# Products of the level scheme as two 64x64 blocks on column halves, and the samples' state updates by head on four row groups

## The chip, the core and the metric

The kernel runs on one core of a Trainium2 chip as one launch. The metric is the device time of the run in microseconds. TensorE multiplies, VectorE, ScalarE and GpSimd do the elementwise work, SyncE issues most of the transfers. SBUF holds 128 partitions; products land in eight PSUM banks of 512 float32 columns.

## What is computed

One step of a decoder layer for 512 prompt tokens and 8 samples of 4 tokens (544 tokens of width 1024), all in float32: a token mixer (a recurrent HGRN2 part of 4 heads and a short gated convolution, from one input projection), a normalisation, a mixture of 16 experts with two experts per token, and a normalisation. The recurrence, per head with keys and values of 128:

```python
S_t = diag(f_t) S_{t-1} + k_t v_t^T
o_t = S_t^T q_t
```

It is evaluated in chunks. The attention inside a chunk needs the product of decayed queries and keys for all causal pairs of tokens, and the state at the end of a chunk needs the sum of the decayed keys times the values. The samples start from given states, 8 x 4 matrices of 128x128, and return new ones.

## The kernel before

Every engine runs its own instruction list, written out by hand; semaphores order them. No planner is involved: the order of the work is the order in the source.

**Input projection with the level products.** The input weight comes in 14 chunks of 256 columns (`ORDER`: f, f, q, q, v, v, gc, gc, cx, cx, gb, gb, g, g). Each chunk is split into a high and a low part (ScalarE line 776, VectorE line 1073) and multiplied (lines 1644, 1651, 1652). Between the projections stand the pair products (`pairs`, lines 1667 to 1687). A prompt chunk has 128 tokens; the causal pairs of a chunk are split by binary levels. Level product 0 gives the diagonal; product `li` from 1 to 7 gives the pairs that lie in the two halves of a block of 2^li tokens, with queries and keys decayed to the middle of the block. Each is computed as a full 128x128 product for each of 4 heads and 4 chunks, and VectorE keeps what the level's mask selects (`take_pairs`, line 1136, a predicated copy). A head's four products fill one bank, and banks 4, 5 and 6 rotate: line 1683 waits until the head three places before was taken. Product `li` runs after projection `li + 4`.

The exponents of a level are made by GpSimd (lines 626 and 627), which waits until the products of the levels before are through, ScalarE exponentiates them (line 826), and VectorE multiplies them into the queries and keys (lines 1123 and 1124) behind the taking of the pairs and the split of the next weight chunk. In the steps of the chunks cx and gb VectorE also evacuates the projection's tiles (lines 1094 to 1114): a cx tile takes the whole convolution. In a VectorE step the order is: evacuate the projection two steps back, take the pairs, split the weights, multiply the decays.

After the last level the keys are decayed to the ends of their chunks (GpSimd line 636, ScalarE line 835, VectorE line 1180) and transposed by TensorE (lines 1717 and 1720); for the samples four transposes, one for each head, lay the 32 tokens on partitions 0 to 31.

**Output, mix and state updates.** The mixer's outputs are normalised per tile of 128 tokens and multiplied by the output weight in two halves of 512 columns, each in a convolution part and a recurrent part (`mix`, lines 1785 to 1806; the tile `tt = 4` holds the 32 sample tokens). The samples' state updates stand between the recurrent parts of the first half (lines 1828 to 1832). For head `h`, GpSimd spreads the values of the 32 sample tokens over 8 blocks, one for each sample, masked to that sample's rows (`mask_values`, line 658); TensorE multiplies the 32 key rows by four blocks at a time into banks 1 and 2 (line 1814), and VectorE adds the products to the decayed states (`new_states`, line 1280). There is one buffer of masked values, so the mask of the next head waits for the products of the one before (line 667). VectorE's order is: add the mix tile to the residual with its statistics, split weights where they are due (after tile 1), new states of the head. After the new states SyncE stores them (line 513) and goes on to the experts' weights. The second half of the mix (`last_mix`), the normalisation, the router and the experts follow.

## Time and profile before

| | |
|---|---|
| Time before, median of 3 runs | 677.18 us (675.67 to 677.30) |
| Profiled execution: its own time | 673.15 us |
| Profiled execution: span | 671.3 us |
| Mean granted TensorE clock | 0.985 |
| TensorE busy | 641.9 us, 96% of the span |
| VectorE busy | 513.9 us, 77% |
| ScalarE busy | 351.5 us, 52% |
| GpSimd busy | 147.1 us, 22% |

The profile is one execution. Times in rows are microseconds from the start of the span unless marked ns. PE is TensorE's matmul side, PEld its weight loads, DVE is VectorE, ACT ScalarE, POOL GpSimd, SP SyncE. A row names the line of the kernel, the operation, output and input, and the shape; `x32` counts records. A float32 product makes two matmul records, a transpose or a product of split (float32r) operands one. The projections take the span up to about 237 us, the mixer's outputs and the mix run to about 317, routing to about 350, the experts to about 660.

### The profile page before, as it was taken

The numbers are of one execution on the slowest core, as the hardware profiler recorded it, in microseconds if no ns is written. First come the engines' busy times: TensorE is split into PE (matmuls) and PEld (weight loads), VectorE is DVE, ScalarE is ACT, GpSimd is POOL, SyncE is SP. The second block draws the span as 40 slices with busy tenths as digits, with TensorE's granted clock in tenths as the row PEclk, the third lists the DMA queues.
The fourth block names the chain that finished last, engine by engine and source line by source line (L and its number), as shares of the span: only waits on it lengthen the run. The fifth ranks groups of instructions, "written<-read, shape, count | busy, mean of one in ns | idle before, by whom it ended". The sixth has DMA issues, their size and how long they took to land.

```text
span 671.3 us, 9632 instructions
## 1 busy us (share of the span) xinstructions
PE 641.9 (96%) x3809; PEld 544.5 (81%) x3809; DVE 513.9 (77%) x599; ACT 351.5 (52%) x353; POOL 147.1 (22%) x81
## 2 busy tenths in 40 slices
PE   8999999988999999999979999999999999999894
PEld 6999899988997897578857888888888888888641
DVE  4326446699767376877679999999999999999887
ACT  4538423322226162012506877877777777777732
POOL 0000514422221330400020211122212222200657
PEclk9999999999999999999779999999999999999998
DMA  9972112111612205089249999999999999998443
GB/s 289 380 291 64 63 63 64 63 63 63 188 63 63 85 17 201 0 276 410 75 148 351 355 411 408 414 418 395 413 412 406 409 419 406 401 413 326 137 164 133
DMA packets 48994, 163.16 MB, mean 243 GB/s; under 512 B 4342, under 2 KB 23626, under 8 KB 36668
## 3 DMA queue, kind: packets, MB, share of 16 engines
q1 hardware_dynamic: 42092, 137.22, 54.0%
q0 software_dynamic: 6864, 25.43, 10.0%
q8 instruction: 25, 0.41, 0.3%
q14 instruction: 13, 0.11, 0.0%
HBM read 142.67 MB, written 19.96 MB: 242 GB/s over the span
## 4 chain that ended last, share of the span: by engine, by line
PE 86%; DVE 8%; ACT 2%; POOL 1%; issue 1%; DMA 1%; SPq 0%; DVEq 0%
PE bank L1922 25%; PE bank L1934 13%; PE bank L1651 7%; PE bank L1652 7%; PE bank L1804 5%; PE bank L1644 5%; PE bank L1686 4%; PE bank L1912 2%; PE bank L2026 1%; PE bank L1884 1%; PE bank L1839 1%; PE bank L1944 1%; PE bank L1814 1%; PE bank L2038 1%; PE bank L1615 1%; PE bank L1616 1%
## 5 line engine op out<-in xcount | busy, mean ns | idle before, releaser
L1439 DVE TENSOR_TENSOR RA<-FA,RA 128x2048 fp32r<-128x2048 f32 x93 | 212.7, 2289 | 20.8 <-ACT RA L929 20.2
L929 ACT ACTIVATE RA<-FA 128x2048 fp32r<-128x2048 f32 x93 | 179.0, 1925 | 41.5 <-PE bank L1922 25.5
L1922 PE MATMUL bank<-RA 128*128 128x512 f32 x768 | 184.9, 395 | 2.9 <-DVE RA L1444 2.0
L1922 PEld LDWEIGHTS bank<-RA 128*128 128x128 f32 x768 | 141.0, 188 | 34.0 <-DVE RA L1444 2.4
L1651 PE MATMUL bank<-RA 128*128 128x272 f32 x432 | 109.1, 290 | 0.0
L1652 PE MATMUL bank<-RA 128*128 128x272 f32 x432 | 108.5, 288 | 0.0
L1934 PE MATMUL bank<-RA 128*128 128x512 f32 x384 | 89.9, 390 | 1.4 <-DVE RA L1449 1.4
L1934 PEld LDWEIGHTS bank<-RA 128*128 128x128 f32 x384 | 72.0, 188 | 16.6 <-DVE RA L1449 1.6
L1651 PEld LDWEIGHTS bank<-RA 128*128 128x128 f32 x432 | 81.5, 189 | 0.0
L1652 PEld LDWEIGHTS bank<-RA 128*128 128x128 f32 x432 | 81.4, 188 | 0.0
L1073 DVE TENSOR_TENSOR RA<-FA,RA 128x2048 fp32r<-128x2048 f32 (+1 forms) x18 | 48.6, 2699 | 26.6 <-ACT RA L776 26.2
L776 ACT ACTIVATE RA<-FA 128x2048 fp32r<-128x2048 f32 (+1 forms) x18 | 33.6, 1868 | 50.0 <-PE bank L1652 26.3
L673 POOL DMA_INDIRECT FA<-x_by_token,ids x16 | 39.1, 2447 | 74.8 <-DVE ids L1397 58.4
L690 POOL DMA_DIRECT2D y_by_slot<-FA x14 | 8.1, 579 | 212.0 <-DVE FA L1456 212.0
L1644 PE MATMUL bank<-RA 128*128 128x256 f32 x384 | 47.1, 283 | 0.0
L1644 PEld LDWEIGHTS bank<-RA 128*128 128x128 f32 x384 | 46.1, 188 | 1.2 <-issue 0.7
L1804 PE MATMUL bank<-RA 128*128 128x512 f32 x192 | 47.0, 398 | 0.0
L1804 PEld LDWEIGHTS bank<-RA 128*128 128x128 f32 x192 | 35.5, 188 | 10.2 <-issue 2.3
L626 POOL TENSOR_TENSOR FA<-FA 128x1024 f32<-128x1024 f32 (+1 forms) x7 | 16.6, 2368 | 109.1 <-PE bank L1686 65.8
L826 ACT ACTIVATE FA<-FA 128x2048 f32<-128x2048 f32 (+1 forms) x7 | 13.6, 1947 | 49.4 <-POOL FA L627 49.4
L1686 PE MATMUL bank<-FA 128*128 128x128 f32 x256 | 30.7, 277 | 3.9 <-DVE FA L1136 3.9
L1686 PEld LDWEIGHTS bank<-FA 128*128 128x128 f32 x256 | 29.4, 192 | 4.4 <-DVE FA L1136 4.3
(271 smaller groups left out, 800.8 us busy)
## 6 DMA issues: line engine op xcount, KB each, us to landing
FA<-w_up SPq DMA_DIRECT2D x32, 1024.0 KB, 7.4
FA<-w_gate SPq DMA_DIRECT2D x32, 1024.0 KB, 7.0
FA<-w_down SPq DMA_DIRECT2D x32, 1024.0 KB, 7.9
FA<-w_in SPq DMA_DIRECT2D x13, 1024.0 KB, 5.1
y_by_slot<-FA POOLq DMA_DIRECT2D x14, 512.0 KB, 7.6
y_by_slot<-FA POOLq DMA_DIRECT2D x1, 5120.0 KB, 21.6
FA<-w_out SPq DMA_DIRECT2D x4, 1024.0 KB, 5.1
FA<-x_prompt SPq DMA_DIRECT2D x8, 256.0 KB, 5.1
```

The costliest lines, as they stand in the source:

```text
L673: pool.indirect_dma_start(out=xg[par], out_offset=None, in_=x1_dram, in_offset=bass.IndirectOffsetOnAxis(ap=ids[:, bi:bi + 1].bitcast(U32) ...
L776: nc.scalar.activation(split[o % 2][0][:, cs], raw[o % 3][:, cs], ACT.Copy).then_inc(s_hi, 1)
L929: nc.scalar.activation(split[split_slot(bi, j)][0], raw[place], ACT.Copy).then_inc(m_hi, 1)
L1073: tt_(split[o % 2][1][:, cs], raw[o % 3][:, cs], f(split[o % 2][0][:, cs]), ALU.subtract).then_inc(s_lo, 1)
L1439: tt_(sl[1], raw[place], f(sl[0]), ALU.subtract).then_inc(m_lo, 1)
L1644: last = mm(pb[:, 0:CW], xT[x_][:, kt, tok(j)], w_[:, kt, :], start=(kt == 0 and i == 0), stop=(kt == KT - 1 and i == 2))
L1651: mm(pb[:, 0:HT], lhs, xT[x_][:, kt, 0:HT], start=first, stop=end)
L1652: last = mm(ps[:, 0:HT], lhs, xT[x_][:, kt, HT:T], start=first, stop=end)
L1686: last = mm(bank[4 + p % 3][:, cols], lf[:, h, cols], rf[:, h, cols], start=True, stop=True)
L1804: last = mm(w_bank(half, tt)[0:rows, :], xT[x_][:, k0 + kt, tok(tt)], w_[:, kt, :], start=(conv and kt == 0 and i == 0), stop=(not conv an ...
L1922: last = mm(out[:, :], xgT[par][x_][:, kt, :], w[w_][:, t, :], start=(kt == 0 and i == 0), stop=(kt == KT - 1 and i == 2))
L1934: last = mm(bank[5 + g][:, :], hT[x_][:, kt, :], w[w_][:, t, 512 * g:512 * g + 512], start=(kt == 0 and i == 0), stop=(kt == 3 and i == 2))
```

## The change

The level products 1 to 6 are made of two 64x64 products per chunk: the first 64 tokens against themselves, written to partitions 0 to 63, and the last 64, written to partitions 64 to 127. Product 7 is one 64x64 product (first half's keys, second half's queries). Product 0 is unchanged. What is not written in the bank is not selected by the masks.

The samples' keys and values are laid out by head on four groups of 32 partitions: the decayed sample keys are multiplied into a separate buffer (`k_end`), so that one transpose turns all heads; ScalarE copies the values of heads 1 to 3 to partitions 32 to 127; one masking instruction on GpSimd covers all heads. The eight products of the update (head `n % 4`, sample half `n // 4`) go to banks 1, 2 and 6 in turn and are issued in groups of 3, 3 and 2 after the mix tiles 1, 2 and 3. TensorE gets two new waits: for all tiles of the mixer's output before the first group, and for six of the new states before the second half of the mix, which uses bank 6.

```diff
--- before.py
+++ after.py
@@ -111,7 +111,7 @@
     c[:, C_IO:C_IO + P] = np.arange(P)[None, :]
     s[:, SM_G4:SM_G4 + TOPG] = TOPG - np.arange(TOPG)
     s[:, SM_VAL:SM_VAL + NTT] = (np.arange(NTT)[None, :] * P + p[:, None]) < T
-    s[:, SM_SEQ:SM_SEQ + DB] = (p[:, None] // DS) == np.arange(DB)[None, :]
+    s[:, SM_SEQ:SM_SEQ + DB] = (p[:, None] % NS // DS) == np.arange(DB)[None, :]
     c[:, C_QM:C_QM + DB * NS] = (np.arange(NS)[None, :] // DS == np.arange(DB)[:, None]).reshape(1, -1)
     m = np.zeros((P, LEVELS, P), np.float32)
     for l in range(LEVELS):
@@ -187,7 +187,7 @@
 
         k_tok = fa(E0 + H * T, H * NC * P).rearrange("p (h c k) -> p h c k", h=H, c=NC)
         state = fa(E0, NC * H * P).rearrange("p (c h v) -> p c h v", c=NC, h=H)
-        k_tok_s = fa(Q0 + H * T, 512).rearrange("p (h k) -> p h k", h=H)
+        k_tok_s, k_end = fa(Q0 + H * T, P), fa(E0 + H * T + H * NC * P, P)
         v_msk = fa(Q0 + H * T + 512, DB * P).rearrange("p (b v) -> p b v", b=DB)
         h_gain, h_gain_s = fa(Q0 + H * T + 1536, 512), fa(Q0 + H * T + 2048, P)
         B0 = Q0 + 2 * H * T
@@ -247,7 +247,7 @@
         s_kt, s_ktc = sem("k_transposed"), sem("k_token_major")
         s_su, s_st, s_o = sem("state_update"), sem("state_ready"), sem("o_made")
         s_x2, s_fold = sem("x_tail_ready"), sem("tail_rows_folded")
-        s_vm, s_sus, s_s0n, s_sto = sem("v_masked"), sem("sample_update"), sem("sample_state"), sem("sample_states_stored")
+        s_vm, s_sus, s_s0n, s_sto = sem("v_by_head_and_masked"), sem("sample_update"), sem("sample_state"), sem("sample_states_stored")
         s_stp = sem("prompt_state_stored")
         s_selt, s_sel = sem("groups_transposed"), sem("groups_t_ready")
         s_csq, s_cms, s_crt, s_crc, s_cbc = (sem("conv_squares"), sem("conv_mean_square"), sem("conv_root"),
@@ -377,6 +377,12 @@
         def o_width(tt):
 
             return H * P if tt < 4 else P
+
+        UPDATE_UNITS = (range(0, 3), range(3, 6), range(6, 8))
+
+        def update_bank(n):
+
+            return bank[(1, 2, 6)[n % 3]]
 
         def w_bank(half, tt):
 
@@ -652,20 +658,14 @@
             pool.wait_ge(s_eva, len(act_tiles) + 1)
             nc.gpsimd.tensor_tensor(sg[:, 4, 0:P], sg[:, 4, 0:P], h_gain_s, ALU.mult).then_inc(s_sg, 1)
 
-            seq_mask = small[0:NS, SM_SEQ:SM_SEQ + DB].unsqueeze(2).broadcast_to([NS, DB, P])
-
-            def mask_values(h):
-                nc.gpsimd.tensor_tensor(v_msk[0:NS], v_tok[0:NS, 4, h * P:(h + 1) * P].unsqueeze(1).broadcast_to([NS, DB, P]),
-                                        seq_mask, ALU.mult).then_inc(s_vm, 1)
-
+            seq_mask = small[:, SM_SEQ:SM_SEQ + DB].unsqueeze(2).broadcast_to([P, DB, P])
             pool.wait_ge(s_fold, 2)
-            mask_values(0)
+            pool.wait_ge(s_vm, 1)
+            nc.gpsimd.tensor_tensor(v_msk, v_tok[:, 4, 0:P].unsqueeze(1).broadcast_to([P, DB, P]), seq_mask,
+                                    ALU.mult).then_inc(s_vm, 1)
             pool.wait_ge(s_stp, 16)
             pool.wait_ge(s_o, NTT)
             nc.gpsimd.memset(xr[:, 4, :], 0.0).then_inc(s_xr0, 1)
-            for h in range(1, H):
-                pool.wait_ge(s_sus, 2 * h)
-                mask_values(h)
 
             def gather(bi, par):
 
@@ -825,6 +825,10 @@
                     n = T if l < SLEVELS else SEQ
                     nc.scalar.activation(ex[l % 2][:, :, 0:n], ex[l % 2][:, :, 0:n], ACT.Exp).then_inc(s_e, 1)
                 if o == 9:
+                    act.wait_ge(s_fold, 2)
+                    for h in range(1, H):
+                        last = nc.scalar.activation(v_tok[h * NS:(h + 1) * NS, 4, 0:P], v_tok[0:NS, 4, h * P:(h + 1) * P], ACT.Copy)
+                    last.then_inc(s_vm, 1)
                     act.wait_ge(s_selt, 1)
                     act.wait_ge(s_b, H)
                     nc.scalar.activation(const[0:8, C_RST:C_RST + 4 * P], bank[7][0:8, :], ACT.Copy).then_inc(s_sel, 1)
@@ -1177,13 +1181,14 @@
                     nc.vector.tensor_copy(p_decay, ex[1][:, :, P - 1:SEQ:P])
                     link(nc.vector.tensor_copy(s0_decay.rearrange("p (b h) -> p h b", h=H), ex[1][:, :, SEQ + DS - 1:T:DS]))
                     dve.wait_ge(s_e, LEVELS + 2)
-                    tt_(k[:, :, :], k[:, :, :], ex[0][:, :, :], ALU.mult).then_inc(s_kx, 1)
+                    tt_(k_end.rearrange("p (h t) -> p h t", h=H), k[:, :, SEQ:T], ex[0][:, :, SEQ:T], ALU.mult)
+                    tt_(k[:, :, 0:SEQ], k[:, :, 0:SEQ], ex[0][:, :, 0:SEQ], ALU.mult).then_inc(s_kx, 1)
 
                     for h in range(H):
                         dve.wait_ge(s_kt, h + 1)
                         nc.vector.tensor_copy(k_tok[:, h, :, :], bank[4 + h % 2][:, :].rearrange("p (c k) -> p c k", c=NC)).then_inc(s_ktc, 1)
                     dve.wait_ge(s_kt, H + 1)
-                    nc.vector.tensor_copy(k_tok_s[0:NS], bank[4][0:NS, :].rearrange("p (h k) -> p h k", h=H)).then_inc(s_ktc, 1)
+                    nc.vector.tensor_copy(k_tok_s, bank[4][:, 0:P]).then_inc(s_ktc, 1)
 
             dve.wait_ge(s_crt, 2)
             nc.vector.reciprocal(r_conv, r_conv).then_inc(s_crc, 1)
@@ -1271,14 +1276,15 @@
                 nc.vector.bn_stats(stats[:, tt, 6 * half:6 * half + 6], xr[:, tt, cols]).then_inc(s_dv, 1)
                 chain[0] += 1
 
-            def new_states(h):
-
-                for g in range(2):
-                    dve.wait_ge(s_sus, 2 * h + g + 1)
+            def new_states(units):
+
+                for n in units:
+                    h, g = n % H, n // H
+                    dve.wait_ge(s_sus, n + 1)
                     for i in range(4):
                         bi = 4 * g + i
                         last = stt(s0[:, bi, h, :], s0[:, bi, h, :], s0_decay[:, bi * H + h:bi * H + h + 1],
-                                   bank[1 + g][:, i * P:(i + 1) * P], ALU.mult, ALU.add)
+                                   update_bank(n)[:, i * P:(i + 1) * P], ALU.mult, ALU.add)
                     last.then_inc(s_s0n, 1)
 
             dve.wait_ge(s_o, NTT)
@@ -1290,8 +1296,8 @@
                 add_mix(0, tt)
                 if tt == 1:
                     lo(NCH + 2)
-                if tt < H:
-                    new_states(tt)
+                if tt in (1, 2, 3):
+                    new_states(UPDATE_UNITS[tt - 1])
             lo(NCH + 3)
             dve.wait_ge(s_lnp, 32)
             for tt in range(NTT):
@@ -1681,9 +1687,17 @@
                     p = li * H + h
                     if p >= 3:
                         pe.wait_ge(s_pc, p - 2)
+                    to = bank[4 + p % 3]
                     for c in range(NC):
                         cols = slice(c * P, (c + 1) * P)
-                        last = mm(bank[4 + p % 3][:, cols], lf[:, h, cols], rf[:, h, cols], start=True, stop=True)
+                        first, second = slice(c * P, c * P + P // 2), slice(c * P + P // 2, (c + 1) * P)
+                        if li == 0:
+                            last = mm(to[:, cols], lf[:, h, cols], rf[:, h, cols], start=True, stop=True)
+                        elif li < LEVELS:
+                            mm(to[0:P // 2, first], lf[:, h, first], rf[:, h, first], start=True, stop=True)
+                            last = mm(to[P // 2:P, second], lf[:, h, second], rf[:, h, second], start=True, stop=True)
+                        else:
+                            last = mm(to[0:P // 2, second], lf[:, h, first], rf[:, h, second], start=True, stop=True)
                     last.then_inc(s_p, 1)
 
             for o_ in range(NCH):
@@ -1716,8 +1730,7 @@
                             for c in range(NC):
                                 last = tr(bank[4 + m % 2][:, c * P:(c + 1) * P], k[:, m, c * P:(c + 1) * P], ident)
                         else:
-                            for h in range(H):
-                                last = tr(bank[4][0:NS, h * P:(h + 1) * P], k[:, h, SEQ:T], ident)
+                            last = tr(bank[4][:, 0:P], k_end, ident)
                         last.then_inc(s_kt, 1)
 
                     pe.wait_ge(s_csq, 1)
@@ -1805,13 +1818,15 @@
                                   start=(conv and kt == 0 and i == 0), stop=(not conv and kt == 3 and i == 2))
                 last.then_inc(s_w, 1)
 
-            def sample_updates(h):
-
-                pe.wait_ge(s_vm, h + 1)
-                for g in range(2):
-                    if h:
-                        pe.wait_ge(s_s0n, 2 * h + g - 1)
-                    mm(bank[1 + g][:, :], k_tok_s[0:NS, h, :], v_msk[0:NS, 4 * g:4 * g + 4, :],
+            def sample_updates(units):
+
+                pe.wait_ge(s_vm, 2)
+                pe.wait_ge(s_ol, NTT)
+                for n in units:
+                    if n >= 3:
+                        pe.wait_ge(s_s0n, n - 2)
+                    rows, g = slice((n % H) * NS, (n % H + 1) * NS), n // H
+                    mm(update_bank(n)[:, :], k_tok_s[rows, :], v_msk[rows, 4 * g:4 * g + 4, :],
                        start=True, stop=True).then_inc(s_sus, 1)
 
             pe.wait_ge(s_cl, 5)
@@ -1828,8 +1843,8 @@
             for tt in range(NTT):
                 pe.wait_ge(s_ol, tt + 1)
                 mix(0, False, tt)
-                if tt < H:
-                    sample_updates(tt)
+                if tt in (1, 2, 3):
+                    sample_updates(UPDATE_UNITS[tt - 1])
 
             def logits(tt):
 
@@ -1860,6 +1875,7 @@
                     pe.wait_ge(s_wc, tt)
                 mix(1, conv, tt)
 
+            pe.wait_ge(s_s0n, 6)
             for n in range(6):
                 last_mix(n)
             pe.wait_ge(s_s0n, 2 * H)
```

## Rows read from the trace of the kernel before

**Rows 1.** The page: busy time of the engines; granted TensorE clock in 40 slices.

```profile
PE 641.9 (96%) x3809; PEld 544.5 (81%) x3809; DVE 513.9 (77%) x599; ACT 351.5 (52%) x353; POOL 147.1 (22%) x81
...
PEclk9999999999999999999779999999999999999998
```

**Rows 2.** Waits of TensorE, 60 to 345 us: total us, times, longest us.

```profile
PE bank L1686 <- DVE FA L1136: 3.9, 2, 2.0
...
PE bank L1637 <- ACT FA L788: 2.0, 2, 1.6
```

**Rows 3.** Chain that ended last, 90 to 345: start us, us, engine, line, records.

```profile
110.25 0.37 PE bank L1679 x8
110.62 3.77 PE bank L1686 x32
...
126.41 3.57 PE bank L1686 x32
...
147.07 1.16 PE bank L1686 x8
...
214.26 0.61 PE bank L1720 x4
...
247.44 1.88 PE bank L1782 x64
```

**Rows 4.** Timeline of TensorE's weight loads, 246.5 to 250: start us, us, line, shape.

```profile
247.01 0.15 PEld L1779 LDWEIGHTS bank<-FA 32*32 32x32 f32 x8
```

**Rows 5.** Timeline of VectorE, 76 to 250: start us, us, [idle before, releaser].

```profile
127.34 0.74 DVE L1136 COPY_PREDICATED FA<-masks,bank 128x512 f32<-128x512 uint8 x1 [4.62 <-PE bank L1686]
...
130.79 3.45 DVE L1073 TENSOR_TENSOR RA<-FA,RA 128x2048 fp32r<-128x2048 f32 x1
...
142.51 0.06 DVE L1094 MEMSET FA<- 128x2 f32 x1 [0.45 <-PE bank L1652]
...
146.30 2.71 DVE L1136 COPY_PREDICATED FA<-masks,bank 128x512 f32<-128x512 uint8 x4
...
179.01 0.74 DVE L1136 COPY_PREDICATED FA<-masks,bank 128x512 f32<-128x512 uint8 x1
...
212.07 1.29 DVE L1184 COPY FA<-bank 128x512 f32<-128x512 f32 x2 [3.80 <-PE bank L1717]
```

**Rows 6.** Timeline of ScalarE, 76 to 250.

```profile
142.54 1.91 ACT L776 ACTIVATE RA<-FA 128x2048 fp32r<-128x2048 f32 x1 [4.12 <-PE bank L1652]
...
203.38 2.03 ACT L835 ACTIVATE FA<-FA 128x2176 f32<-128x2176 f32 x1 [5.78 <-POOL FA L636]
...
240.58 1.27 ACT L854 ACTIVATE FA<-FA 32x128 f32<-32x128 f32 x4
```

**Rows 7.** Timeline of VectorE, 246 to 328, at the state updates.

```profile
272.87 0.69 DVE L1266 SCALAR_TENSOR_TENSOR FA<-FA,bank 128x512 f32<-128x512 f32 x1 [1.44 <-PE bank L1804]
...
274.20 2.27 DVE L1073 TENSOR_TENSOR RA<-FA,RA 128x2048 fp32r<-128x2048 f32 x1
276.39 2.15 DVE L1280 SCALAR_TENSOR_TENSOR FA<-FA,bank 128x128 f32<-128x128 f32 x8
```

**Rows 8.** Chain that ended last, 90 to 345, state updates and mix.

```profile
267.92 1.91 PE bank L1814 x4
...
283.24 1.91 PE bank L1814 x4
...
287.14 16.70 PE bank L1804 x72
```

**Rows 9.** Stretches of 1 us: length, busy us by engine, clock, DMA share, GB/s.

```profile
335.00:336.00 1.00, 0.54 (x3) 0.12 (x1) 0.86 (x5) 0.00 (x0) 0.00 (x0) 1.00 0.00 0
337.00:338.00 1.00, 0.13 (x5) 0.13 (x5) 1.00 (x4) 0.00 (x0) 0.00 (x0) 0.76 0.00 0
339.00:340.00 1.00, 0.95 (x11) 0.90 (x12) 0.37 (x2) 0.00 (x0) 0.00 (x0) 0.50 0.00 0
344.00:345.00 1.00, 1.00 (x5) 0.82 (x4) 1.00 (x2) 0.00 (x0) 1.00 (x1) 0.83 0.82 283
```

## The prediction

> **What bounds the kernel now.** I read the page first: TensorE is busy for 96% of the span, no other engine for more than 77%, and the granted clock is full except in one stretch near the middle [rows 1]. So I looked for the places where TensorE waits ahead of the expert loop. There are few: twice about 2 us in the level products, on VectorE's taking of the level before, and 1.6 us on a ScalarE evacuation [rows 2]. The chain of waits through both changed stages is therefore made of TensorE's own instructions, and work taken from them comes off the end unless VectorE is late next. That question decides the sum.
>
> A float32 product shows as two matmul records. A head of a level (four 128x128 products) is 8 records, a level 32 records in 3.57 us, 112 ns each [rows 3]. Products of 32 columns to the four column groups of one bank run closer: 64 records in 1.88 us, 29 ns each, although each streams the same 128 columns [rows 3]. Four column groups of one row group thus run side by side.
>
> **Part 1, the level products.** Levels 1 to 6 now issue two 64x64 products per chunk, 64 records; the last level one, 32 records; the diagonal stays. No row shows 64 columns. From below, a record streams half of 128 columns, 56 ns, and two halves side by side give 28 ns a record, nearly what the four groups show. From above, records of 32 columns that all go to one column group take 0.37 us for 8, 46 ns [rows 3]; twice the columns would be 92 ns. I take 29 ns, because the nearest rows alternate column groups as the change does, and their weight loads overlap too: eight loads to four groups of one row group lie within 0.15 us [rows 4]. A level is then 64 x 29 ns = 1.88 us. The last one sends 32 records to one half, so I take 56 ns each, 1.8 us.
>
> The Trainium skill, TensorE: Matmul & The Clock Gate, section on packing small matmuls, has weight loads overlap running matmuls only where the row group differs, which the two halves do not. The overlapping loads above speak against it; by that rule the sum would be the slower rival below.
>
> Now VectorE. Three banks rotate, so TensorE's fourth head waits until VectorE has taken the first.
> - Products 1 to 3. VectorE starts its first take 0.04 us after the first head's 8 x 112 ns [rows 3, 5], later about 0.6 us after the level's start; TensorE resumed 0.77 us after such a take began (146.30 to 147.07 [rows 3, 5]). The fourth head may start at 1.37, before the third ends (1.41). A level is 1.9 us, a gain of 1.65, three times: 4.95. VectorE's four takes, 0.68 each back to back, end 1.0 us earlier, and it had 0.45 us to spare ahead of the next tile [rows 5], about covering the 1.65.
> - Products 4 and 5 follow the cx tiles. VectorE is still on the convolution there, runs without a gap, and TensorE stands before the fourth head. Only that head shrinks, 1.16 to 0.74 us with its drain [rows 3]: 0.42 twice, 0.84.
> - Products 6 and 7 follow the gb tiles; the first take starts when VectorE is through them (179.01 [rows 5]), the fourth head at 179.78, the end at 180.25. Now such a level starts 0.93 us before its first take (126.41 and 127.34 [rows 3, 5]), so it ends at 179.01 - 0.93 + 3.57 = 181.65: 1.4 twice, 2.8.
>
> That is 8.6. Changing the product's width may cost something: levels that follow 32-column products show 3.77 against 3.57 [rows 3]. Between 0 and 0.2 us for seven levels I take 0.15, 1.0 in all. **7.6 us** are left.
>
> Behind the last level GpSimd's subtraction starts; ScalarE's exponential waits 5.78 us for it, then squares, and only then evacuates the tile for which TensorE waited 1.6 us [rows 2, 6]. This chain moves with TensorE. GpSimd is slowed while VectorE splits weights beside it (both then stretch: 3.45 us for a split [rows 5], 2.27 elsewhere [rows 7]), and it now has some 0.6 us more ahead of that split, since VectorE is still taking pairs: between 0 and 0.6, I take **0.4**. Four transposes of sample keys become one; three fewer at 0.11 (0.61 for four, with a lead-in [rows 3]) give **0.3**. VectorE multiplies the 128 sample columns apart from the rest: one instruction more, hidden because VectorE then waits 3.80 us for TensorE's transposes of the result [rows 5]; without that cover some 0.2. ScalarE's three copies of values (four like them took 1.27 us [rows 6], so about 1.0) sit in its queue before the copy of the group table and the weight rounding of the next chunk; there it waits 4.12 us for a cx tile [rows 6], so nothing, and at most 1.0 without that. GpSimd's wait for them ends long before it gets there.
>
> **Part 2, the state updates.** Now each head costs TensorE 1.91 us for two products [rows 8], four times. Between the first update's start, 267.92, and the second half of the mix, 287.14, lie 19.2 us. The first mix tile (12 records in 2.78 us, as 72 in 16.70 [rows 8]) would end at 270.7, no update ahead of it. Three products on three row groups follow. No row shows row groups side by side; alone a product is 0.95, so three lie between 0.95 and 2.85; I take 1.05, because the column groups overlap fully: 271.75. The next mix ends at 274.55. Then VectorE is late: sum and statistics 1.33 us, a weight split 2.19, and 1.07 for a unit's four state rows (2.15 for eight) [rows 7]. From 270.75 the first three units are free at 275.35, 276.4 and 277.5. The next three products want those banks, so they go one by one to 278.55. A new wait of about 0.8 us arises before the first, with the next mix queued behind it. Mix to 281.35, two products 1.0, the short tail tile 2.0 (283.24 + 1.91 to 287.14 [rows 8]): the second half starts at 284.35, **2.8 us** earlier. Its new wait, on six units, ends near 282.2. The weights for its third tile are split by about 290, when they are needed: this is late next. GpSimd's 3 masks are gone; one with 128 partitions takes its first one's place ahead of the residual's loads. The new wait for all mixer rows is over before the first mix tile ends. The state store, on SyncE's queue ahead of the expert weights, moves earlier by about 1 us, less than what reads them, but they are wanted only after the routing.
>
> **The clock.** In the two cx levels TensorE finishes three heads in 1.4 us instead of 2.7 and stands still for some 3.2 us instead of 2.0. In the routing it now idles from about 335.5; within 337 to 338 the granted clock falls (0.76 on average) to the lower of its levels, 0.50 or 1.2 GHz; dense work runs from about 339.5, and full speed, 2.4 GHz, comes back in 344 to 345 [rows 9]. Some 5 us of dense work at half speed lose 2.5 us. The two gaps of 2.0 us in the levels did not drop it [rows 1]. Between no drop and two (0 and 5.0) I take one: **-2.5**.
>
> **The sum.** 7.6 + 0.4 + 0.3 + 2.8 - 2.5 = 8.6 us. Against the profiled run's own 673.15 us (span 671.3) that is 664.55. The median shown, 677.18, stands 4.0 above that run; the predicted median is 677.18 - 8.6 = 668.6.
>
> **The rivals.**
> - The halves follow one another, loads hidden: four records of 56 ns a chunk, 224, as now. Levels 1 to 6 gain nothing, no gap grows, only the last level's 1.4 stays: 1.4 + 0.4 + 0.3 + 2.8 = 4.9, 672.3. Against it: 29 ns in [rows 3]. 0.10.
> - Slower: the halves share one row group, the load of the second cannot start under the first, and every record costs 92 ns. A level of 64 records is 5.9 us, 2.3 more. Four levels (1, 2, 3 and 6) bound by TensorE give 9.2, the fourth heads of the two cx levels 2 x 0.6, the last level (2.9) gains 0.6; less 3.5 from the rest: 6.3 slower, 683.5. It decides from about 70 ns a record, where the levels' loss eats the 3.5. For it: 46 ns in one column group; against it: the overlapping loads [rows 4]. 0.04.
> - The row groups do not overlap: 1.05 + 2.85 - 2.1, about 1.7 less from the updates: 670.3. 0.08.
> - The clock falls in more places (both gaps, the wait in the updates, and beyond): four falls of 2.5 leave 11.1 - 10 = 1.1 us, 676.1, no measurable change. 0.05.
> - The change does not do what it says, the stage being set by VectorE throughout: the 0.45 us that VectorE has to spare in one place and the 4.62 in another [rows 5] speak against that. Only the updates gain: 674. 0.03.
>
> **How the numbers follow.** The forecast, with none to two falls, has 0.70. 0.3% of 677.18, about what a measurement of this kernel can tell from no change, is 2.0 us. Faster: the forecast, the hidden-load case, the row groups and most of the last case, 0.90; same 0.06; slower 0.04. The range: no fall and no cost of width give 11.1 + 1.0 = 12.1, 665.1, and the runs spread 1.5 below their median, so 664.0; at the top 672.3 with the row groups also failing, 674, cut to 673.5.
>
> **What would show it.** Right: records of the level products near 29 ns and levels near 1.9 us; TensorE's wait on VectorE's takes at about 3 us twice; one mask on GpSimd; a wait of about 0.8 us on new states before the fourth update product, and later products one by one; the mix's second half 16.4 us after the first mix tile. Wrong: level products at 3.6 us or more; the granted clock at 0.50 after more than two places; TensorE waiting for cx or gb evacuations where it ran through; the second half waiting for its weights.

## The result, and the profile after

The changed kernel takes 670.17 us in the median of four runs (669.29 to 671.23), the kernel before beside it 677.05 (675.67 to 677.30): 6.9 us less. The ratio is 0.9909, with an interval of 0.9884 to 0.9934, which is 4.5 to 7.9 us. The forecast was 8.6 less, 668.6 us; the time is in its range, though 8.6 itself lies above that interval. One execution of the experiments below, of the kernel with the updates alone, took 1059.89 us at a granted clock of 0.555 and enters no ratio.

The two profiled executions are closer than the medians: 671.23 us (span 669.4) after and 673.15 (span 671.3) before. A second profile of the kernel before, from the experiments below, is longer: 677.22 us (span 675.4). First the page of the kernel after, TensorE's busy time and its granted clock in 40 slices:

```profile
PE 638.1 (95%) x3998; PEld 539.6 (81%) x3998; DVE 510.1 (76%) x600; ACT 352.7 (53%) x356; POOL 138.8 (21%) x78
...
PEclk9999999978999999899789999999999999999997
```

The busy shares are within a point of those of before, but the clock is now below full in two places ahead of the slice where it fell before [rows 1]. The level products come next: the line view of the kernel after, first the two halves of level 1 in a window around it, then the last level, which has one half (record durations min/median/max in ns, first and last start in us).

```profile
L1697 PE MATMUL bank<-FA x32: 222/222/271, 95.2 to 97.2; 128*64 128x64 f32 x32
...
L1700 PE MATMUL bank<-FA x32: 222/222/270, 192.8 to 194.8; 128*64 128x64 f32 x32
```

In level 1 the other half's 32 records (line 1698) lie between these: 64 records start within 2.0 us, 32 ns apart. In the last level 32 records that all go to one half start within the same 2.0 us, 64 ns apart. So two halves take the time of one. The 32 and 64 ns are means. The timelines of level 1 show what is in them, first TensorE's records (start, duration), then VectorE's takes:

```profile
95.72 0.22 PE L1697 MATMUL bank<-FA 128*64 128x64 f32 x1
95.73 0.22 PE L1698 MATMUL bank<-FA 128*64 128x64 f32 x1
95.78 0.22 PE L1697 MATMUL bank<-FA 128*64 128x64 f32 x1
...
96.60 0.22 PE L1698 MATMUL bank<-FA 128*64 128x64 f32 x1
96.75 0.27 PE L1697 MATMUL bank<-FA 128*64 128x64 f32 x1
```

```profile
95.94 2.61 DVE L1140 COPY_PREDICATED FA<-masks,bank 128x512 f32<-128x512 uint8 x4 [0.18 <-PE bank L1698]
```

In a run a pair of records, one for each half, starts every 58 ns, which is 29 ns a record. The fourth head starts at 96.75, 0.15 us behind the last record of the third and 0.81 us after VectorE's first take began. On the chain, level 1 lasts from 95.28 to 97.43, 2.15 us, against 3.57 to 3.77 before [rows 3]. This is what TensorE waits for:

```profile
PE bank L1697 <- DVE FA L1140: 6.2, 2, 3.1
...
PE bank L1643 <- ACT FA L788: 1.9, 2, 1.6
...
PE bank L1829 <- DVE FA L1286: 0.8, 1, 0.8
```

The two waits on VectorE's takes have grown from 3.9 us in all [rows 2] to 6.2, 3.1 each; the wait on ScalarE's evacuation has stayed; the wait on new states is new and has the 0.8 us forecast. The chain of the kernel after, in the stretches that the change touches:

```profile
192.83 2.22 PE bank L1700 x32
...
212.03 0.33 PE bank L1733
...
262.60 5.59 PE bank L1817 x24
...
272.99 3.10 PE bank L1829 x6
276.09 4.54 PE bank L1817 x12
280.63 1.06 PE bank L1829 x4
...
283.68 16.69 PE bank L1817 x72
```

One transpose of sample keys stands where four did [rows 3]; three products on three row groups, 268.10 to 269.17 in the trace, take 1.07 us, then VectorE is late and the next three go one by one in 3.10. The mix tile behind them takes 4.54 us for 12 records; the first two tiles, 24 records at 262.60, take 5.59, 2.8 each. The 1-us stretches say why (columns: busy shares of PE, PEld, DVE, ACT and POOL with their records, granted clock, DMA share, GB/s):

```profile
143.00:144.00 1.00, 0.24 (x4) 0.24 (x6) 1.00 (x4) 0.00 (x0) 0.00 (x0) 0.66 0.00 0
...
149.00:150.00 1.00, 1.00 (x7) 1.00 (x6) 1.00 (x2) 0.00 (x0) 1.00 (x1) 0.50 0.00 0
...
276.00:277.00 1.00, 1.00 (x4) 0.84 (x4) 1.00 (x5) 0.00 (x0) 0.00 (x0) 0.72 0.00 0
...
279.00:280.00 1.00, 1.00 (x4) 0.77 (x3) 0.33 (x2) 0.00 (x0) 0.00 (x0) 0.57 0.00 0
```

Towards the end of each 3.1-us wait the clock falls from full (2.4 GHz) to 0.50 (1.2 GHz). Worked out from the means of the first and last stretch of each fall, it is low from 143.3 to 150.1, from 163.8 to 167.2 and from 276.4 to 279.9; the last lies within the mix tile just named, with TensorE busy.

To see where the time went, I cut every trace at the first starts of the same lines, read to 0.1 us: product 0's sample part, the transposes behind product 3 and behind product 7, the first prompt state update, the samples' outputs, the first transpose of the normalised residual, the first transpose of gathered tokens. Microseconds from each cut to the next, the last one to the end of the span:

| stretch | before | before again | after |
|---|---|---|---|
| start to product 0 | 76.6 | 76.9 | 77.4 |
| products 0 to 3 | 53.2 | 53.3 | 49.1 |
| products 4 to 7 | 67.3 | 68.8 | 68.5 |
| behind product 7 | 39.9 | 39.9 | 39.5 |
| prompt states | 10.4 | 10.4 | 10.4 |
| outputs, mix, updates | 56.3 | 57.8 | 55.3 |
| residual to routing | 44.6 | 44.6 | 46.1 |
| experts and rest | 323.0 | 323.7 | 323.1 |

Products 0 to 3 gain 4.1 us, nearly the 4.5 worked out. Products 4 to 7, which should gain 3, lose 1.2 us against the first profile, and the updates give 1.0 instead of 2.8. Both are where the clock fell.

### The profile page after: what moved, and what is told of

It reads as the page before. It is cut to its first block, busy times and chain, and to the rows that moved or that the text cites. A ratio compares the mean times of both kernels' runs of the same rounds, so it can differ in the third digit from the quotient of the medians.

```text
span 669.4 us, 10013 instructions
## 1 busy us (share of the span) xinstructions
PE 638.1 (95%) x3998; PEld 539.6 (81%) x3998; DVE 510.1 (76%) x600; ACT 352.7 (53%) x356; POOL 138.8 (21%) x78
## 4 chain that ended last, share of the span: by engine, by line
PE 83%; DVE 9%; ACT 3%; POOL 2%; DMA 1%; issue 1%; SPq 1%; DVEq 0%
PE bank L1938 25%; PE bank L1950 13%; PE bank L1657 8%; PE bank L1658 7%; PE bank L1817 6%; PE bank L1650 4%; PE bank L1928 2%; PE bank L1854 2%; PE bank L1697 1%; PE bank L2042 1%; PE bank L1960 1%; PE bank L1900 1%; PE bank L2054 1%; DMA FA<-x_prompt 1%; PE bank L1621 1%; POOL FA L642 1%
## 5 line engine op out<-in xcount | busy, mean ns | idle before, releaser
L1938 PEld LDWEIGHTS bank<-RA 128*128 128x128 f32 x768 | 141.0, 188 | 34.1 <-DVE RA L1450 2.4
L1657 PE MATMUL bank<-RA 128*128 128x272 f32 x432 | 112.2, 295 | 0.0
L1658 PE MATMUL bank<-RA 128*128 128x272 f32 x432 | 111.2, 293 | 0.0
L1950 PEld LDWEIGHTS bank<-RA 128*128 128x128 f32 x384 | 73.1, 191 | 17.0 <-DVE RA L1455 1.6
L1657 PEld LDWEIGHTS bank<-RA 128*128 128x128 f32 x432 | 83.8, 194 | 0.5
L1658 PEld LDWEIGHTS bank<-RA 128*128 128x128 f32 x432 | 83.7, 194 | 0.0
L673 POOL DMA_INDIRECT FA<-x_by_token,ids x16 | 39.5, 2469 | 107.1 <-DVE ids L1403 91.6
L776 ACT ACTIVATE RA<-FA 128x2048 fp32r<-128x2048 f32 (+1 forms) x18 | 33.6, 1867 | 50.6 <-PE bank L1658 27.7
L1650 PEld LDWEIGHTS bank<-RA 128*128 128x128 f32 x384 | 46.1, 188 | 1.2 <-issue 1.2
L1817 PEld LDWEIGHTS bank<-RA 128*128 128x128 f32 x192 | 36.6, 194 | 10.0 <-issue 1.5
L632 POOL TENSOR_TENSOR FA<-FA 128x1024 f32<-128x1024 f32 (+1 forms) x7 | 16.6, 2368 | 107.5 <-PE bank L1698 64.2
L938 ACT ACTIVATE RA<-bank 128x512 fp32r<-128x512 f32 x32 | 17.2, 593 | 16.3 <-PE bank L1928 16.3
L1140 DVE COPY_PREDICATED FA<-masks,bank 128x512 f32<-128x512 uint8 x28 | 18.4, 727 | 9.3 <-PE bank L1698 9.3
```

The costliest lines, as they stand in the source:

```text
L673: pool.indirect_dma_start(out=xg[par], out_offset=None, in_=x1_dram, in_offset=bass.IndirectOffsetOnAxis(ap=ids[:, bi:bi + 1].bitcast(U32) ...
L776: nc.scalar.activation(split[o % 2][0][:, cs], raw[o % 3][:, cs], ACT.Copy).then_inc(s_hi, 1)
L1140: nc.vector.copy_predicated(att[:, h, :, :], m, src).then_inc(s_pc, 1)
L1650: last = mm(pb[:, 0:CW], xT[x_][:, kt, tok(j)], w_[:, kt, :], start=(kt == 0 and i == 0), stop=(kt == KT - 1 and i == 2))
L1657: mm(pb[:, 0:HT], lhs, xT[x_][:, kt, 0:HT], start=first, stop=end)
L1658: last = mm(ps[:, 0:HT], lhs, xT[x_][:, kt, HT:T], start=first, stop=end)
```

## The experiments

The theory: the parts do what the forecast says, and the falls of the clock take it back, above all those that the two longer waits bring. The rivals: the halves cost more than their records show, or the falls cost nothing, since other engines set the end of these levels. A gain below is one less the ratio, times the median of the kernel before as measured beside it; by this measure the change itself gains 6.2 us.

### Fill the two waits

TensorE makes twelve products that nothing reads, into the idle bank 7, ahead of the fourth head of products 4 and 5.

```diff
+                    if h == 3 and li in (4, 5):
+                        pe.wait_ge(s_sel, 1)
+                        filler = RA[:, 32 * K + KT * T:32 * K + KT * T + 640]
+                        for _ in range(12):
+                            mm(bank[7][:, :], filler[:, 512:640], filler[:, 0:512], start=True, stop=True)
                     if p >= 3:
```

> The changed kernel, with 12 products of no use (512 columns, into the idle bank 7) ahead of the fourth head of level products 4 and 5, where TensorE otherwise stands for 3.1 us. Theory 'clock': the gaps are what drops the granted clock there (6.4 and 3.3 us at the lower level in the changed kernel's profile, some 3.2 + 1.6 us lost); with the gaps filled the clock stays full from 130 to 180 us, the projections behind levels 4 and 5 start no later than 0.3 us after VectorE's first take, and the run is some 4 to 5 us faster than the changed kernel (670.2), so 665 to 666. Rival 'VectorE': that stretch is as long as VectorE needs, whatever the clock; then the run stays within 1 us of 670.

Measured: 665.42 us, ratio 0.9833 [0.9810, 0.9856], a gain of 11.3 us, 4.8 us under the median of the change. In its 1-us stretches, at the place of the first wait:

```profile
143.00:144.00 1.00, 0.93 (x5) 0.43 (x3) 0.97 (x5) 0.00 (x0) 0.00 (x0) 1.00 0.00 0
144.00:145.00 1.00, 0.93 (x18) 0.86 (x19) 1.00 (x3) 0.00 (x0) 0.15 (x1) 1.00 0.00 0
```

The clock stays full through all levels. Products 4 to 7 take 64.3 us instead of 68.5: the edit adds work to TensorE and takes none away, and the stretch is 4.2 us shorter. The two falls were the cause. The fall in the updates is still there (271.2 to 278.0; that stretch takes 57.0), and is not touched by this edit.

### Each part alone, and the halves in turn

Three kernels, measured together with the last one: the kernel before with only the level products of the change; the change with the level products of before (the loop of four 128x128 products per head); and the change with all first halves of a head ahead of all second halves:

```diff
                         elif li < LEVELS:
-                            mm(to[0:P // 2, first], lf[:, h, first], rf[:, h, first], start=True, stop=True)
-                            last = mm(to[P // 2:P, second], lf[:, h, second], rf[:, h, second], start=True, stop=True)
+                            last = mm(to[0:P // 2, first], lf[:, h, first], rf[:, h, first], start=True, stop=True)
...
+                    if 0 < li < LEVELS:
+                        for c in range(NC):
+                            second = slice(c * P + P // 2, (c + 1) * P)
+                            last = mm(to[P // 2:P, second], lf[:, h, second], rf[:, h, second], start=True, stop=True)
```

> The kernel before with the 64x64 level products alone (the state updates as before). Theory 'clock': levels 1 to 3 take 2.15 us each instead of 3.6 to 3.8, the clock falls in the two gaps, 8 us gained and up to 5 lost: 3 to 5 us faster than before, 672 to 674. Rival: the gain of the change came from the updates alone; then within 1 us of 677.

> The changed kernel with the level products as full 128x128 blocks again, so that the state updates alone are changed. Theory 'clock': the updates give 2.8 us (16.4 us from the end of the first recurrent mix tile to the second half of the mix, 19.2 before) where the clock holds through VectorE's wait and the three products one by one, and 1.0 where it falls there as in the changed kernel: 1 to 3 us faster than before, 674 to 676. Rival 'levels alone': no gain, within 1 us of 677.

> The changed kernel, with the four products of a head's first half issued before the four of its second half (levels 1 to 6), the same products in another order. Theory 'side by side': halves overlap only where they alternate; a record then takes 56 ns or more and a level 3.6 us, as in the kernel before, the gaps in levels 4 and 5 shrink to about 2 us, and the levels' gain is gone: 672 to 675. Rival 'shorter products': a level stays near 2.15 us, because 64 columns stream faster than 128, and the time stays at 670.

Measured: the levels alone 669.73 us, ratio 0.9905 [0.9875, 0.9936], a gain of 6.4; the updates alone 670.76, 0.9926 [0.9899, 0.9952], 5.0; the halves in turn 669.79, 0.9917 [0.9887, 0.9946], 5.6. All three gain more than I expected. By stretch:

| stretch | levels only | updates only | halves in turn | gaps filled |
|---|---|---|---|---|
| products 0 to 3 | 49.1 | 53.3 | 50.6 | 49.0 |
| products 4 to 7 | 65.8 | 68.8 | 68.4 | 64.3 |
| behind product 7 | 39.8 | 39.6 | 39.5 | 39.5 |
| outputs, mix, updates | 57.8 | 53.8 | 53.8 | 57.0 |

The chain of the kernel with the updates alone, at the place shown above for the change:

```profile
267.04 5.58 PE bank L1809 x24
...
277.43 3.10 PE bank L1821 x6
280.52 2.98 PE bank L1809 x12
283.51 1.06 PE bank L1821 x4
...
286.56 15.55 PE bank L1809 x67
```

The same products, and the mix tile now takes 2.98 us: where the clock holds, the updates gain 2.5 (53.8 against 56.3), here and in the halves in turn. Where it falls beside the old updates, as with the levels alone (from 275 on) and in the second profile of before, the stretch is 57.8, and the gain against that would be 4.0. The parts together gain less than the two alone (6.2 against 6.4 + 5.0); in the profiles each of the two was spared a fall that the whole has. Elsewhere in this profile the updates alone gain only 0.3, behind product 7; their 5.0 [3.2 to 6.8] is more than these 2.8 together. That the old updates often meet a fall, and so lose more than the first profile shows, would explain it, but how often was not measured.

The levels alone show that a long wait does not bring a fall every time. Their profile has the same two waits as the change (140.35 to 143.43 and 157.88 to 160.96); a line of its waits and a 1-us stretch behind the first:

```profile
PE bank L1691 <- DVE FA L1136: 6.2, 2, 3.1
```

```profile
144.00:145.00 1.00, 1.00 (x11) 0.96 (x8) 1.00 (x2) 0.00 (x0) 0.79 (x1) 1.00 0.00 0
```

The clock stays full behind the first wait and is low only behind the second, from 162.5 to 165.9; products 4 to 7 take 65.8 us, 1.5 more than with the gaps filled, where the two falls of the change cost 4.2. In the profile of the updates alone, with the waits of before (2.0 us), it is low from 148.7 to 152.1, behind the first of them.

The halves in turn missed what I expected. Its line view, level 1:

```profile
L1697 PE MATMUL bank<-FA x32: 221/222/272, 95.6 to 97.8; 128*64 128x64 f32 x32
L1703 PE MATMUL bank<-FA x32: 221/222/271, 95.8 to 98.1; 128*64 128x64 f32 x32
```

64 records start within 2.5 us, about 40 ns apart, though eight in a row go to the same half; one half alone has 64 ns in the mean. The start of its timeline there:

```profile
95.55 0.50 PE L1697 MATMUL bank<-FA 128*64 128x64 f32 x5
95.84 0.27 PE L1703 MATMUL bank<-FA 128*64 128x64 f32 x1
95.89 0.22 PE L1697 MATMUL bank<-FA 128*64 128x64 f32 x1
```

In the list of instructions the second half's first record (line 1703) stands behind eight of the first half; in the trace it starts behind five, ahead of the sixth. They overlap without being issued one by one in turn, at a price: 0.5 us a level, 1.5 for three levels (50.6 against 49.1). What in the engine lets them is not shown by any of these runs. The whole comes out at the time of the change: in its profile the waits are shorter (2.6 us), the falls in the levels too (146.2 to 149.6 and 166.7 to 170.1), and the updates are spared.

### Two groups of four updates

With the gaps filled, the updates go in two groups of four row groups, to banks 1, 2, 6, 7 and 1, 2, 4, 5; the second group stands behind the mix's tail, its new states behind the last weight split.

```diff
-        UPDATE_UNITS = (range(0, 3), range(3, 6), range(6, 8))
+        UPDATE_UNITS = (range(0, 4), range(4, 8))
...
-            return bank[(1, 2, 6)[n % 3]]
+            return bank[(1, 2, 6, 7, 1, 2, 4, 5)[n]]
...
             lo(NCH + 3)
+            new_states(UPDATE_UNITS[1])
...
-                if tt in (1, 2, 3):
-                    sample_updates(UPDATE_UNITS[tt - 1])
+                if tt in (1, 4):
+                    sample_updates(UPDATE_UNITS[tt // 4])
```

> The changed kernel with the two gaps of the level products filled, and with the eight update products in two groups of four, all four row groups at once: the first four behind the second recurrent mix tile (banks 1, 2, 6, 7), the other four behind the tail tile (banks 1, 2, 4, 5), the new states of the second four behind the last weight split. Theory 'banks': TensorE's wait of 0.8 us and the three products one by one (3.1 us) come from having three banks; with four and five a group takes 1.1 us, nothing waits, the second half of the mix starts some 13 us after the end of the first recurrent mix tile (16.5 in the changed kernel at full clock), so 2 to 4 us faster than with the gaps filled alone (665.4): 661 to 664. Rival 'VectorE': the new states only move behind the split, the normalisation waits for VectorE, and the time stays at 665.

Measured: 660.28 us, ratio 0.9775 [0.9743, 0.9806], a gain of 15.2, 3.9 more than with the gaps filled alone. Its chain:

```profile
258.45 5.57 PE bank L1823 x24
264.01 1.07 PE bank L1836 x8
...
272.69 1.09 PE bank L1836 x8
273.79 16.91 PE bank L1823 x72
```

Four products cost what three cost (1.07), none waits, and no fall comes before 310. The stretch of the mix and updates takes 49.8 us, 4.0 less than the 53.8 of the three-group order where the clock holds. Between the end of the first mix tile (258.45 and half of 5.57) and the second half lie 12.6 us: three tiles at 2.8 to 2.9, the tail 1.8, and 2.2 for all eight products. The updates alone had 16.7 there (269.83 to 286.56): the difference is VectorE's being late, the wait and the products one by one.

### Four banks for the levels; the kernel before with its gaps filled; the kernel before again

Four banks instead of fillers, with the updates in two groups as before: products 4 to 6 rotate over banks 4 to 7, so that the fourth head no longer waits.

```diff
+        def pair_bank(p):
+
+            return bank[4 + (p % 4 if 4 * H <= p < 7 * H else p % 3)]
```

The filled kernel before has the filler of the first experiment with seven products instead of twelve, for its shorter waits; the third kernel is the one before, unchanged.

> The updates as in the run with two groups, and no filler: instead the level products 4 to 6 rotate over four banks (bank 7 too), so that TensorE need not wait for VectorE's first take. Theory 'clock and VectorE': the 3.1 us gaps go, and the next projection starts 3 us earlier, but VectorE is busy without a break in the two cx steps, so TensorE waits elsewhere (for an evacuated cx tile, for decays), some 2 us twice; the stretch to the end of level 7 gets 1 to 3 us shorter than with filled gaps where the clock holds: 659 to 664. Rival: the waits only move and drop the clock as before: 664 to 667.

> The kernel before, with 7 products of no use ahead of the fourth head of level products 4 and 5, where its gaps are 2.0 us. Theory 'clock': its profile shows full clock there, but other executions may have lost it (the updates alone, with the same level products, showed one fall of 3.4 us there): 0 to 3 us faster than before, 674 to 677, and full clock from 130 to 180 us. Rival: the clock is no matter in the kernel before: within 1 us of 677.

> The kernel before, once more, for a second profile of it. Theory 'clock': the one profile shown is one of its faster executions (673.15 against a median of 677); a second one shows the clock falling in places where the first does not, in the gaps of the level products, the updates or the last experts, some 1.7 us for each. Rival: the same falls as in the first, and the profile's own time near 673.

Measured with four banks: 659.05 us, ratio 0.9754 [0.9724, 0.9785], a gain of 16.6. The two waits are gone without fillers, but another has come in their place. The largest of TensorE's waits:

```profile
PE bank L1709 <- DVE FA L1132: 3.9, 2, 3.7
```

Two 1-us stretches of the same kernel, in that wait and at its end:

```profile
169.00:170.00 1.00, 0.00 (x0) 0.00 (x0) 1.00 (x2) 1.00 (x1) 0.00 (x0) 1.00 0.00 0
...
171.00:172.00 1.00, 0.20 (x4) 0.20 (x6) 1.00 (x2) 0.00 (x0) 0.00 (x0) 0.50 0.63 238
```

TensorE now stands 3.7 us before product 6, until VectorE has multiplied its decays, and the clock falls there, from 170.2 to 177.0. Products 4 to 7 take 63.8.

The kernel before with its gaps filled: 674.53 us, ratio 0.9997 [0.9975, 1.0019]. No change that can be measured: products 4 to 7 take 67.3, as in the first profile. Filling pays where waits bring the clock down. Those of 2.0 us did not in the first profile; in the profile of the updates alone and in the next one a fall stands behind one of the two. What that leaves to gain on average is within the interval, from 1.3 us lost to 1.7 gained.

The kernel before again: 675.73, ratio 0.9996 [0.9967, 1.0026], single runs 671.69 to 679.49. In its profile the clock is low in three places where the first profile of before has it full, 166.2 to 169.6, 282.3 to 285.7 and 640.7 to 644.1; stretches from the first two:

```profile
168.00:169.00 1.00, 1.00 (x6) 1.00 (x6) 1.00 (x1) 0.00 (x0) 1.00 (x2) 0.50 0.00 0
...
283.00:284.00 1.00, 1.00 (x4) 0.78 (x3) 0.85 (x4) 0.00 (x0) 1.00 (x1) 0.50 0.00 0
```

Each of these two cost 1.5 us (68.8 against 67.3, and 57.8 against 56.3 in the table), and the last stretch, with the third, is 0.7 longer: 3.7 of the 4.1 us between the two profiled executions. So falls come in some executions of the kernel before and not in others, and the profile on which the prediction stood was one with few. That explains most of the 4.0 us by which it lies under its median. The first pair of profiles shows 1.9 us where the medians show 6.9 for this reason and because the profiled execution of the change was the slowest of its four, 1.1 above their median.

### Four banks, and the new wait filled

```diff
+                    if li == 6:
+                        pe.wait_ge(s_pc, 6 * H)
+                        filler = RA[:, 32 * K + KT * T:32 * K + KT * T + 640]
+                        for _ in range(13):
+                            mm(bank[7][:, :], filler[:, 512:640], filler[:, 0:512], start=True, stop=True)
                     pe.wait_ge(s_z, li)
```

> The run with four banks, with 13 products of no use ahead of level product 6, where TensorE stands for 3.7 us and the granted clock fell for 6.8 us behind it. Theory 'clock': the fall goes, the end of level 7 comes 2 to 3 us earlier (112.8 us after the start of level product 0 in the run with four banks, 110 to 111 here), and the run takes 656 to 657.5 us against 659. Rival 'VectorE': that stretch is bound by VectorE whatever the clock, the end of level 7 stays, and the time stays at 659.

Measured: 656.22 us (655.75 to 658.04), ratio 0.9716 [0.9690, 0.9741], a gain of 19.2: the best of all, ahead of both kernels. The wait before product 6 is down from 3.7 us to 0.8 and the fall there is gone; from the waits of TensorE:

```profile
PE bank L1714 <- DVE FA L1132: 0.8, 1, 0.8
```

Products 4 to 7 take 61.5 us, 2.3 less than with four banks alone (63.8); the gains differ by 2.6. The first fall of the clock is at 307.

## Why the prediction was right or wrong

- **The level products: right.** I took 29 ns a record from the column groups of 32, and in a run it is 29. With the 0.15 us for the change of width a level was to be 2.03, and is 2.15. That the 0.15 nearly fits is partly luck, since no run shows a cost of width by itself, and about half of what was added comes with the fourth head. I let it start 1.37 us into the level, without a pause; it starts at 1.55 (95.20 to 96.75), after a pause of 0.15, which fits VectorE's first take, begun 0.74 us into the level and not 0.6. The 46 ns behind the slower rival were a mean of eight records; in the trace the last seven of them start 32 ns apart. The last level was to be 1.95 with its width and is 2.22 on the chain: 58 ns a record in a run, not 56, and a pause of 0.21 before its fourth head. Products 1 to 3 were to gain 4.5 with the width taken off (4.95 - 0.45) and gain 4.1; 4 to 7 were to gain 3.0 (0.84 + 2.8 - 0.6) and gain 3.0 where the clock holds (67.3 to 64.3). 7.1 to 7.2 against 7.6. The rivals in which the halves go one after another, or all loads are exposed, are out. The Trainium skill, TensorE: Matmul & The Clock Gate, section on packing small matmuls, lets loads overlap running products only where the row group differs. By it two halves would cost twice one half; the trace disagrees, 32 ns a record with two halves against 64 with one.
- **Behind the last level: half right.** The transposes came (0.33 instead of 0.61). The 0.4 on GpSimd's subtraction did not: its two instructions take 6.01 us in both kernels. I also put TensorE's wait in the wrong place: the 1.6 us on ScalarE [rows 2] stand before product 0, at 73.0 to 74.6. Behind the last level TensorE waits much less for ScalarE, here in windows of 190 to 220, before and after:

```profile
PE bank L1637 <- ACT FA L788: 0.4, 1, 0.4
```

```profile
PE bank L1643 <- ACT FA L788: 0.3, 1, 0.3
```

The stretch goes from 39.9 to 39.5, 0.4 for a forecast of 0.7: 0.28 from the transposes and 0.13 from this wait (0.43 to 0.30).
- **The copies and the split multiplication: right, hidden.** ScalarE's three copies took 0.95 us at 134.60, beside a wait. VectorE's extra multiplication took 0.29 at 203.63; VectorE waits 3.7 us behind it.
- **The updates: right in the mechanism, 2.5 for 2.8.** Row groups overlap (1.07 for three, I took 1.05), the wait is 0.8, the products behind it go one by one, and the second half starts 16.7 us after the first mix tile where the clock holds (the updates alone), for 16.4 forecast and 19.2 before. In the profiled execution of the change only 1.0 of it was left, because the clock fell within a mix tile.
- **The clock: the step that failed.** I took one fall of 2.5 us between none and two, because the 2.0-us waits of before had not dropped it. In the profiled execution of the change both of the new 3.1-us waits dropped it, and the two together cost 4.2 us, as the filled kernel shows; with the levels alone the same two waits brought one fall and 1.5 us. So the length of a wait does not settle whether the clock falls. A third fall, in the updates, cost 1.5 in this execution, beside products that kept TensorE busy; I had no term for it. With three places ahead of the routing at 0.50, a sign that I had named for being wrong came true. The bound of 5.0 held for the levels, but not the value.
- **The reference for the sum.** I took the difference from the profiled run and carried it to the median, as if the two differed by a constant. They differ by falls, which are part of what the change moves. In medians the change gains 6.9: of the terms without the clock, 4.1 + 3.0 + 0.4 + 2.5 = 10.0 for the forecast 11.1, some 3 are given back. Against the profiled run the sum gave 664.55, and the profiled execution of the change took 671.23, 6.7 more. That the median came within 1.6 us of the forecast is therefore partly luck: the kernel before loses to falls in its median too, which the sum did not know. The case of more falls, at 676.1 with a chance of 0.05, was the right direction and too far.

Which executions have a fall, in the levels or in the updates, what starts it in the updates with TensorE busy, and what moves the falls in the routing (317 in the change, 323 before) and near 635, was not tried and stays open. The stretch that holds the former is 1.5 us longer in the profile of the change (46.1 against 44.6).

## What to carry to other kernels

Price a change that makes TensorE faster twice: by what it saves, and by the waits that it lengthens, since a wait can lower the clock for work that the change does not touch, in some executions and not in others. Where a wait cannot be removed, products that nothing reads can hold the clock; where a spare bank removes it, look for the wait that takes its place. Profile the kernel before more than once before its falls, or their absence, go into a sum.

## What the runs showed that was not expected

VectorE and GpSimd do not slow one another a little, as I had read [rows 5, 7]; by the rows below they take turns. VectorE's timeline in the kernel after, behind the first long wait (start, duration, line, output and input, shapes):

```profile
145.70 3.40 DVE L1077 TENSOR_TENSOR RA<-FA,RA 128x2048 fp32r<-128x2048 f32 x1
149.02 2.91 DVE L1127 TENSOR_TENSOR FA<-FA 128x1024 f32<-128x1024 f32 x1
```

GpSimd's timeline there:

```profile
144.97 1.97 POOL L632 TENSOR_TENSOR FA<-FA 128x1024 f32<-128x1024 f32 x1 [12.35 <-PE bank L1698]
146.91 3.94 POOL L633 TENSOR_TENSOR FA<-FA 128x1024 f32<-128x1024 f32 x1
```

The split ends 2.2 us after GpSimd's first instruction (146.94 to 149.10); GpSimd's second ends 1.75 us after the split (150.85); VectorE's decay ends 1.1 us after that (151.93). Each is close to the length that the instruction has elsewhere, 2.27 [rows 7], 1.89 and 1.21, and 0.1 shorter. The Trainium skill, SBUF — State Buffer, section Who interferes with whom, calls the port pair of the two an exclusive lock held for a whole instruction; these rows agree. With four banks GpSimd's exponents start earlier and meet the convolution in place of the split. VectorE's timeline with four banks:

```profile
141.84 1.96 DVE L1116 SCALAR_TENSOR_TENSOR FA<-FA 128x32 f32<-128x32 f32 x1
143.84 2.31 DVE L1115 SCALAR_TENSOR_TENSOR FA<-FA 128x512 f32<-128x512 f32 x1
...
149.14 2.29 DVE L1081 TENSOR_TENSOR RA<-FA,RA 128x2048 fp32r<-128x2048 f32 x1
151.35 1.22 DVE L1131 TENSOR_TENSOR FA<-FA 128x1024 f32<-128x1024 f32 x1
```

The split and the decay now take their usual 2.29 and 1.22 us, and two instructions of the convolution take 1.96 and 2.31 us instead of 0.25 and 0.75; the first ends at 143.80, with GpSimd's instruction from 141.47 to 143.76. The turns are moved, not saved: 3.3 us there, 2.8 in the change.
